# A scan without its mask product, two barriers less, and an output projection whose token tiles are taken 2, 3, 0, 1

## What is computed

```
zxbcdt = u @ w_in                                    # z 2048 | x 2048, B 1024, C 1024 | dt 32
xbc = silu(causal_depthwise_conv(xbc, conv_w, conv_b))
dt = softplus(dt_raw + dt_bias);  a = -exp(a_log)
# scan over chunks: y_t = sum_{s<=t} C_t.B_s exp(sum_{s<k<=t} da_k) x_s
y = (scan(x * dt, dt * a, B, C) + x * d_skip) * silu(z)
y = y * rsqrt(mean_per_group(y^2) + eps) * norm_w;  return y @ w_out
```

## Time and profile before

| | |
|---|---|
| median of three runs | 2555.54 us |
| the profiled execution | 2556.64 us |
| its span | 2554.9 us |
| PE busy | 2444.5 us, 96% |
| DVE / ACT / POOL busy | 38% / 24% / 59% |
| granted PE clock, mean | 0.977 of full speed |

### The profile page before, as it was taken

How to read it: one execution, slowest core, us unless ns; L and a number is a source line. 1 busy time by engine, 2 the same in 40 slices (tenths; PEclk the granted TensorE clock), 3 DMA queues, 4 the chain that set the end, 5 groups by cost and what they waited for, 6 DMA issues and landing times.

```text
span 2554.9 us, 34335 instructions
## 1 busy us (share of the span) xinstructions
PE 2444.5 (96%) x14186; PEld 1960.1 (77%) x14186; DVE 967.5 (38%) x1545; ACT 612.9 (24%) x1265; POOL 1496.4 (59%) x1396
## 2 busy tenths in 40 slices
PE   8998999999999998999999989998798998999998
PEld 6886778888888886568888876665676786888887
DVE  3545553451151401436304355874632324311113
ACT  2222563020020113832101112345542210210010
POOL 7665665586586665329749655560122763865763
PEclk9999999999999998999999999999897999999999
DMA  5232113243232232113313213130000331432321
GB/s 161 83 91 66 44 48 115 67 132 99 83 108 99 82 100 78 32 34 124 99 61 129 94 44 104 27 107 17 2 3 14 107 95 55 123 95 88 103 83 62
DMA packets 106303, 201.78 MB, mean 79 GB/s; under 512 B 9530, under 2 KB 14628, under 8 KB 106148
## 3 DMA queue, kind: packets, MB, share of 16 engines
q1 hardware_dynamic: 101476, 189.36, 23.8%
q10 hardware_dynamic: 4672, 10.23, 1.3%
HBM read 194.71 MB, written 2.10 MB: 77 GB/s over the span
## 4 chain that ended last, share of the span: by engine, by line
PE 86%; DVE 7%; ACT 3%; POOL 2%; issue 1%; DVEq 0%; DMA 0%; ACTq 0%; POOLq 0%; SPq 0%
PE psum L153 37%; PE psum L294 24%; PE psum L155 7%; PE psum L232 3%; POOL weight_split_ring L431 1%; PE psum L1436 1%; PE psum L1150 1%; PE psum L1444 1%; PE psum L194 1%; PE psum L1463 1%; DVE big L2026 1%; DVE best L2025 1%; PE psum L1121 1%; POOL weight_split_ring L428 0%; DVE big L902 0%
## 5 line engine op out<-in xcount | busy, mean ns | idle before, releaser
L153 PE MATMUL psum<-x_split,weight_split_ring 128*128 128x512 f32 x4128 | 973.6, 395 | 3.9 <-POOL weight_split_ring L431 3.9
L431 POOL TENSOR_TENSOR weight_split_ring<-weight_ring,weight_split_ring 128x512 fp32r<-128x512 f32 (+3 forms) x732 | 954.3, 1325 | 30.5
L153 PEld LDWEIGHTS psum<-x_split,weight_split_ring 128*128 128x128 f32 x4128 | 770.5, 188 | 177.8 <-issue 14.9
L428 POOL TENSOR_SCALAR weight_split_ring<-weight_ring 128x1024 fp32r<-128x1024 f32 (+3 forms) x366 | 394.6, 1078 | 689.4 <-PE psum L294 318.0
L294 PE MATMUL psum<-weight_split_ring,hidden_split 128*128 128x512 f32 x2256 | 531.1, 397 | 8.2 <-DVEq L3146 8.2
L294 PEld LDWEIGHTS psum<-weight_split_ring,hidden_split 128*128 128x128 f32 x2256 | 424.8, 189 | 111.0 <-DVEq L3146 8.6
L155 PE MATMUL psum<-weight_split_ring,x_split 128*128 128x512 f32 x864 | 223.9, 406 | 0.2 <-ACT big L1839 0.2
L155 PEld LDWEIGHTS psum<-weight_split_ring,x_split 128*128 128x128 f32 x864 | 158.0, 191 | 46.2 <-issue 15.4
L727 DVE TENSOR_TENSOR big<-big 128x512 f32<-128x512 f32 x64 | 89.3, 1396 | 175.4 <-ACT big L712 175.4
L712 ACT ACTIVATE big<-psum 128x512 f32<-128x512 f32 x64 | 38.3, 598 | 435.1 <-PE psum L153 378.7
L530 DVE SCALAR_TENSOR_TENSOR residual<-residual,psum 128x512 f32<-128x512 f32 x48 | 32.7, 682 | 237.2 <-PE psum L294 237.2
(11 more groups left out here) (362 smaller groups left out, 2543.3 us busy)
## 6 DMA issues: line engine op xcount, KB each, us to landing
weight_ring<-in_mlp_w SPq DMA_DIRECT2D x128, 512.0 KB, 3.7
weight_ring<-in_w_in SPq DMA_DIRECT2D x92, 512.0 KB, 3.6
weight_ring<-in_w_ffn_in SPq DMA_DIRECT2D x40, 512.0 KB, 3.7
weight_ring<-in_w_out SPq DMA_DIRECT2D x24, 512.0 KB, 3.7
weight_ring<-in_w_ffn_out SPq DMA_DIRECT2D x22, 512.0 KB, 3.7
weight_ring<-in_sb_w_q SPq DMA_DIRECT2D x8, 512.0 KB, 3.7
weight_ring<-in_sb_w_k SPq DMA_DIRECT2D x8, 512.0 KB, 3.8
weight_ring<-in_sb_w_v SPq DMA_DIRECT2D x8, 512.0 KB, 3.8
```

What stands on the lines that cost most here:

```text
L153: mm = pe.matmul(out, wp[:, k, m * P:m * P + rows], xp, start=first, stop=last)
L428: pool.tensor_scalar(part.high[:, 0:nk, 0:n], raw, 1.0, 0.0, ALU.mult, ALU.add).then_inc(self.high_made, 1)
L431: low = pool.tensor_tensor(part.low[:, k, 0:n], raw[:, k, :], part.high[:, k, 0:n].bitcast(F32), ALU.subtract)
```

## The change

- `mamba_in` no longer makes the last four tiles (C of groups 4 to 7). They are a Gemm `g2` of their own, taken tile by tile (`by_tile`), and its 16 pieces come at the beginning of the scan's stream. PE's stream has 80 pieces now: AHEAD = 6 before the first step, then two in each step and three in the ten steps of LONGER.
- There is no barrier between `mamba_in` and `mamba_core`. PE, POOL and the rest wait for single tiles instead. The PSUM banks are rotated for it (`shift`).
- The mask matmul is gone. ACT takes relu(sum_s - sum_t) in place in PSUM, four times, waits for itself, waits for outputs(i-1), and then makes one exponential of 512 columns. DVE first multiplies C.B with the triangle (`past_cb`, 128 columns, from PSUM) and then the decay matrix with `past_cb`, both in SBUF.
- decays(i+1) is issued before outputs(i), and waits for exp(i).
- The four convolutions of `g2` stand on DVE before step 0 and in steps 1, 3, 4; their four SiLUs on ACT in step 6.
- POOL's chunks come four in seven steps from step 4 on.
- z's groups are complete in steps 10, 17, 24 and 31 instead of 7, 15, 23, 31, and the later work starts behind these. y's transpose 11 moves out of the scan, to behind the first chunk of `mix1`.
- There is no barrier between `finish_merge` and `norm2`. The Project waits for single merged tiles (`s_used`) and for the banks of the last Gemm, takes the token tiles of its head in the order 2, 3, 0, 1, and has a tail of two chunks instead of three.

```diff
 class StateSpaceCore:
+    AHEAD, LONGER = 6, (1, 3, 4, 8, 12, 15, 19, 22, 26, 29)
+    CONVOLVED = {1: 1, 3: 2, 4: 3}
+    LAST_SILU = 6
         def decays(i):
             if i >= 1:
                 pe.wait_ge(self.s_e, i)
-            pe.matmul(bank..., m.ident_r[:, :], across(m.past_r[:, :], HPG), start=True, ...)
             pe.matmul(bank, m.group_r[:, g:g + 1]..., sums, start=True, stop=True).then_inc(self.s_dec, 1)
+        go_on(self.AHEAD)
+        decays(0)
         for i in range(self.STEPS):
-            decays(i)
-            next(pieces)
+            go_on(1)
             products(i)
-            if j >= 1 and p >= NT:
-                self.turn(pe, NT * (j - 1) + p - NT)
-            next(pieces)
+            for k in self.turns(i):
+                self.turn(pe, k)
+            go_on(self.pieces[i] - 1)
+            if i + 1 < self.STEPS:
+                decays(i + 1)
             outputs(i)
         def exp(i):
-            ins = act.activation(m.decay[:, r, :], kit.psum[...], ACT.Exp, bias=m.ncs[:, c, h:h + 1])
+            ins = act.activation(fall, fall, ACT.Relu, bias=m.cs_cols[:, c, h:h + 1], scale=-1.0)
+            ins.then_inc(self.s_fall, 1)
+            act.wait_ge(self.s_fall, i + 1)
+            if i >= 1:
+                act.wait_ge(self.s_y, i)
+            act.activation(m.decay[...], kit.psum[:, self.DECAYS, :], ACT.Exp, scale=-1.0)
         def mix(i):
+            dve.wait_ge(self.s_cb, i + 1)
+            st(dve.tensor_tensor(m.past_cb, kit.psum[:, self.SUMS, 0:P], m.upper, ALU.mult))
             dve.wait_ge(self.s_e, i + 1)
-            dve.tensor_tensor(m.decay, m.decay, across(kit.psum[:, self.SUMS, 0:P], HPG), ALU.mult)
+            dve.tensor_tensor(m.decay, m.decay, across(m.past_cb, HPG), ALU.mult)
-        for i in range(self.STEPS):                       # ScalarE
-            exp(i)
+        for i in range(self.STEPS + 9):
+            if i < self.STEPS:
+                exp(i)
...
+            for k in self.turns(i):
+                high(k)
+            for j, n in self.due(i, 1):                   # squares, squares, inverse, normalise
...
 class Project:
-                for t in range(NT):
+                for t in range(NT) if self.after is None else (2, 3, 0, 1):
 def project_norm(...):
+    g = Project(kit, w, k_tiles, by_column=m.core if late else None, tail=2 if merged else TAIL,
+                after=m.merge_last if merged else None)
-        flowing = ("mamba_core", "mix1", "mlp1", "mix2", "mlp2", "norm2")
+        flowing = ("mamba_in", "mamba_core", "mix1", "mlp1", "mix2", "mlp2", "finish_merge", "norm2")
```

More of the change, by code:

```diff
@@ L3 @@
 from contextlib import ExitStack
+from dataclasses import dataclass
 import numpy as np
@@ L135, in part @@
         tiles, rows = -(-n // P) if self.feature else NT, min(P, n) if self.feature else P
-        for b, (k0, nk) in enumerate(blocks):
-            pe.wait_ge(kit.chunk_split, i + b + 1)
+        order = [(b, m) for m in range(tiles) for b in range(len(blocks))] if self.by_tile else \
+            [(b, m) for b in range(len(blocks)) for m in range(tiles)]
+        for b, m in order:
+            k0, nk = blocks[b]
             w = kit.split_ring[(i + b) % SPLIT]
[L140 to L161, removed]
@@ new lines, in part @@
+            t = tile + m
+            if m == 0:
+                pe.wait_ge(kit.chunk_split, i + b + 1)
+            if b == 0 and t - self.phase0 >= self.banks:
+                pe.wait_ge(kit.tile_free, t - self.banks + 1)
+            out = kit.psum[0:rows, self.bank(t - self.tile0), 0:WIDE if self.feature else n]
+            for k in range(nk):
+                xk = x(k0 + k)
+                pairs = ((w.high, xk.high), (w.low, xk.high), (w.high, xk.low))
+                for q, (wp, xp) in enumerate(pairs):
+                    first = b == 0 and k == 0 and q == 0
+                    last = b == len(blocks) - 1 and k == nk - 1 and q == 2
+                    if self.feature:
+                        mm = pe.matmul(out, wp[:, k, m * P:m * P + rows], xp, start=first, stop=last)
+                    else:
+                        mm = pe.matmul(out, xp[:, m * P:(m + 1) * P], wp[:, k, 0:n], start=first, stop=last)
@@ L163, in stream @@
+            if b == len(blocks) - 1:
+                mm.then_inc(kit.tile_ready, 1)
+            elif m == tiles - 1:
+                mm.then_inc(kit.part_used, 1)
+            yield
     def stream(self, pe, x):
@@ L300, in start_tile @@
         tile = self.tile0 + 2 * t + n
-        if tile - self.phase0 >= BANKS:
+        if self.after is not None:
+            for i in range(self.after.count):
+                if self.after.bank(i) == self.bank(2 * t + n):
+                    self.after.wait_free(pe, i)
+        elif tile - self.phase0 >= BANKS:
             pe.wait_ge(self.kit.tile_free, tile - BANKS + 1)
@@ L767, in more_constants @@
     assert cut.n == CONSTANT_STEPS
+@dataclass
+class Inlet:
+    gemm: object
+    first: int
+    conv: object
+    silu: object
+    start: object
+    s_silu: object
+    s_tf: object
 def mamba_in(nc, kit, m, a):
@@ L954, in vector @@
         for n in range(NT):
-            conv(n)
+            conv(dve, n)
         time_steps()
-        for n in range(NT, XBC_TILES):
+        for n in range(NT, LAST):
             if n == X_TILES + NT:
@@ L2989, in __init__ @@
                              .rearrange("p (c r l) -> p c r l", c=2, r=HPG)]
-        self.past_r = self.hid.low[:, 8, 0:P]
+        self.past_cb = self.part(b, 12288, P)
         self.xring = self.part(b, 8192, 8, SEQ)
```

214 lines of the change are left out of this document (120 added, 94 removed).

## The result

The changed kernel takes 2542.23 us (median of 5 runs, 2539.68 to 2548.61), the kernel before 2555.54 in the same comparison. The ratio is 0.9942, with a 95% interval of 0.9931 to 0.9952: 12 to 18 us less. The forecast was 2536.2 us, so 19.3 us less; the gain came to 13.3 by the medians and to 14.5 by the spans of the two profiled executions (2554.9 and 2540.4 us). The direction was right, the size was 5 to 6 us too large.

A forecast was written before the change was run, and what follows sets the result against it. PE was taken as the bound, busy 2444.5 of 2554.9 us. The terms sum to -19.3, giving a span of 2535.6 and a median of 2536.2 us; own range 2530 to 2542, 8-in-10 range 2527 to 2545.5.

The forecast's parts named there:

- mask matmul: In each of 32 scan steps, removing this matmul saves PE 0.41 us: 13.1 us less.
- first barrier: Between `mamba_in` and the scan: 10.9 us of idle time and slow clock go, 1.2 us stays; gain 9.7 us.
- waits in the steps: In the scan, PE waits for late mixes, folds and `gated`, less two old stalls: net 4.3 us lost.
- end of the scan: Behind the scan, moved transpose 11 delays squares and normalise; PE stalls 3.2 us at transpose 12, clock 0.8: 4.0 us lost.
- second barrier: Between `finish_merge` and norm2: idle time goes, but PE waits 3.8 us for DVE, clock 1.4; gain 5.1 us.
- third pieces, clock and spacing elsewhere: Ten moved pieces between short matmuls or beside others of the scan cost about 0.03 us more each: 0.3 us lost.
- the two old stalls: PE's two old scan waits on `mix`, 0.87 us each, go as the SiLUs' table load moves: 1.7 us back.
- the ten listed steps: Scan steps 5, 6, 11, 13, 14, 20, 21, 27, 28, 30: PE waits 0.45 us each for the mix, 4.5 us.
- The waits of `products` for the fold: In the scan, folds late behind convolutions cost 1.0 us for three steps; `gated` in step 11 costs 0.5 us.
- signs of being wrong: PE waiting on ACT in the steps, a table load each step, a weight-chunk wait, or low clock inside the scan.
- The rival in which DVE sets the scan: In the scan, the product costs 1.53 us every step and folds 3.05: 9 us lost, 2545 us; chance 0.18.
- the rival of relu and the table: In the scan, relu is not in the exponential's table, so each step has two loads: 2562 us; chance 0.04.

The follow-up runs named there:

- three stood together: Changed kernel with sums matmul of 128 rows, transpose 11 behind the second product of `mix1`'s first chunk, and norm2's tail of three chunks: 2527.57 us, ratio 0.9896.

## Why the prediction was right and where it failed

The terms, in us, and what the traces show in their place:

| term | predicted | measured |
|---|---|---|
| mask matmul | -13.1 | -7.4 (32 x 0.23) |
| first barrier | -9.7 | -10.5 |
| waits in the steps | +4.3 | +6.0 |
| end of the scan | +4.0 | +5.2 |
| second barrier | -5.1 | -7.9 |
| third pieces, clock and spacing elsewhere | +0.3 | +0.1 (what is left) |
| sum | -19.3 | -14.5 |

**The mask.** This is the step that failed: "0.41 with the other steps ... 32 of them: 13.1 us less on the path". It took the distance between the mask's start and the next matmul's for what its removal gives. The neighbour changed with it. The sums matmul behind it has 64 rows, and its weight load is not taken ahead. Behind the last product it starts after 0.93 us, where the mask matmul started after 0.81, so that part of its delay had been covered. Taken from the old kernel the mask gave 0.29 us a step, in the new order 0.23. That the order is not the cause was shown by `decays` behind `outputs`, and that the 64 rows are, by the kernel with 128. The Trainium skill (TensorE: Matmul & The Clock Gate, Step-by-step: what each phase is for) says that weight loads are pulled ahead of running matmuls if "the row groups don't conflict" or they go to the background buffer, and that the row count doesn't matter for their time. The load itself agrees (0.18 us with 64 rows, 0.19 with 128); that its height decides whether it is taken ahead stands in the runs here alone.

**The first barrier.** Right. PE goes from product to piece without a wait, `decays(0)` waits for nothing, and the first mix costs 0.4 us instead of 1.2 (from sums matmul to last product 1.37 us, 207.06 to 208.43, one step later 0.97): 10.9 - 0.4 = 10.5. Put back, the barrier costs 12.5 by the ratios, some 3 us to each side, and 11.5 by the trace.

**The steps.** The mechanism was right in the main, the size 1.7 us too small, and one part was wrong. The product takes 1.09 us in the mean (taken: 1.0) between 0.69 and 1.55 (bounds: 0.68 and 1.53). The 14 that took 0.69 us fell where POOL rested; the 18 others, 0.92 to 1.55 us, fell beside POOL's split of a weight chunk (for example 1.45 us at 238.14, with POOL in L442 from 237.72 to 240.71).

PE's 12 waits in the scan are 5.2 us of idle time, but the pipeline makes them dearer. At the wait of 0.62 us it is 1.83 us from the state product to the last product (238.41 to 240.24), where the same pair without a wait is 0.97 apart (219.15 to 220.12): 0.86 us. Counted so from start to start, the 12 cost 7.4 us, each between 0.02 and 0.24 more than its idle time, and four short ones that show no idle time 1.2: 8.6. Less 0.4 for the first, which is booked at the barrier, and 2.2 for the two old stalls by the same reckoning: 6.0.

Where they fell: six of the ten listed steps (5, 6, 13, 20, 27, 30) waited for the mix, 4.5 us together. That is the sum taken, but it was luck: four steps had none, and four had 0.9 to 1.0 us instead of 0.45. The waits of `products` for the fold were taken at 1.0 and 0.5 and came to 2.5 us. And "the two old stalls of 0.87 go ... 1.7 us back" failed in part. ACT still loads a table (1.28 us) ahead of the exponential in five of the 32 steps, and behind two of these loads PE waits for ACT, 0.32 us each, and once more for the mix, 1.2 us from start to start. Waits of PE on ACT were among the signs of being wrong.

The rival in which DVE sets the scan (9 us) did not come: the waits at the mix are seven, of 0.2 to 0.8 us of idle time. The kernel without `past_cb` shows that 3.8 of the 5.2 us come from `past_cb` and the longer product. Nor did the rival of relu and the table: in 27 of the 32 steps no load stands between relus and exponential. Over the whole stretch, from the last product of `mamba_in` to `mix1`, the kernel before took 191.4 us (215.63 to 407.01), the changed one 200.9 (195.1 to 396.04) with 16 pieces more in it (96 matmuls, 21.9 us): 12.4 us gained, where the forecast's terms give 18.2. The mask is 5.7 of the difference and the steps 1.7, while the barrier gave 0.8 more than taken and 0.7 came from the third pieces, from transpose 11, which left the scan, and from rounding.

**The end of the scan.** Right: squares at 7.9 us (predicted 7.7), normalise at 14.8 (14.3), the stall 3.5 (3.2). The clock behind it cost more: from transpose to transpose 4.66 us (414.22 to 418.88) instead of 3.24, so 1.4 and not 0.8. Which clock comes there differs between executions: of the eight traces with 3.0 to 3.5 us of idle time there, one has 3.27 us for this distance and seven have 4.53 to 5.84. From `mix1` to the second late transpose (396.04 to 418.88) it is 22.84 us, where 72 matmuls and one turn took 17.3 at full speed before; 0.36 of the difference is transpose 11 itself, the rest 5.2. Transpose 11 early takes most of both away.

**The second barrier.** The mechanism was right, the size 2.8 us too small. DVE's tail from the same point is 20.8 us long (2145.46 to 2166.27), not 22.3, so PE's wait is 2.44 us and not 3.8. What the prediction left in the tail is DVE's wait of 1.61 us for the deviation, behind ACT's table load; it is 0.27 us now. (Of the two waits that it took off, 1.6 and 1.7 us, the second was for ACT and not for PE.) The other half is luck: no slow clock followed, for which 1.4 had been taken. Of the seven traces with this wait the 24 matmuls behind it took 3.13 or 3.14 us in two and 4.30 to 4.64 in five. From the first of the merge's last 96 matmuls to the feed-forward net it took 79.5 us before (2101.53 to 2181.00) and 71.5 now (2094.87 to 2166.40), 7.9 less. Put back, with the old order and tail, the barrier costs 7.4 by the ratios.

**The rest.** 3 us were lost at 49 us, behind a wait that both kernels have; at the last product of `mamba_in` 1.4 of it is left, by 195.1 against 215.63 - 21.9. Between `mix1` and norm2 1.2 us came back. The terms up to `mix1`, with transpose 11 out of the scan (0.36 us), add up to 12.3 us, 0.1 less than the stretch gained. A third piece costs its step nothing beyond its own 1.37 us, where 0.03 had been taken. A single profiled execution doesn't tell such amounts from chance: the medians differ by 13.3 us, the spans by 14.5.

## What to carry to other kernels

Price the removal of a matmul by what its neighbours will then show, not by its own row: a short one that stands ahead of a weight load which isn't taken ahead is partly free, and the idle time of the row that loads weights says so. Count a wait from the start of one matmul to the start of the next, since here its idle time alone left out two fifths of the cost. A barrier is worth its idle time and the slow clock behind it, less the wait that the next chain needs anyway; look for that chain first, since here a shorter tail and one moved transpose gave back 6 us (2.6 and 3.6) of what was gained elsewhere. Improvements too small for the ratio to resolve were found by the trace, and the ratio showed them when three stood together.

## What the runs showed of the hardware

- A weight load of 64 rows among matmuls of 128 is not taken ahead, and the load behind it isn't either: 0.36 and 0.24 us of idle time on PEld, none with 128 rows, where the upper half is zeros. The 128-row form saved 0.40 us in a step without waits.
- The granted clock after a short idle time isn't the same in each execution. Behind the same 2.83 us it was 1.00 in the kernel before and 0.57 in the changed one, worth 3 us, and over 12 traces the 24 matmuls there took 5.7 us in four and 7.3 to 8.5 in eight. Behind 2.44 us in norm2 24 matmuls took 3.13 us, behind 2.46 in another kernel 4.64. A term of 1 to 3 us for the clock is a chance, not a value.
- A DVE product of 512 columns with both operands in SBUF took 0.69 us while POOL rested and 0.92 to 1.55 us beside POOL's split of a chunk; with one in PSUM it took 0.67 to 0.69 in all 32 steps. The Trainium skill (GPSIMD Engine Reference, Specifications) has the contention, which these rows agree with.
